# A hybrid block with a sparse mixture of experts: tokens sorted on the chip, and two of four tiles combined and gated between the last expert units

## The reference

```
v   = rmsnorm(h)
moe = for each token: the best of 4 groups of experts, in it the best 2 of 8 experts,
      expert(v) = (silu(v @ w_gate) * (v @ w_up)) @ w_down        # 1024 -> 256 -> 1024
      weighted by the group's probability and the two experts' weights
h   = h + moe
gate = sigmoid(rmsnorm(h) @ W_g + b_g)                            # W_g: 1024 x 1024
h   = h + gate * (p @ W_ple)                                      # p: 512 x 256
out = rmsnorm(h)
```

## Time and profile before

| | us |
|---|---|
| median of 3 runs | 517.59 (516.82 to 517.95) |
| the profiled execution's own time | 518.2 |
| its span | 516.5 |
| busy: TensorE / VectorE / ScalarE / GpSimd | 461.3 / 227.3 / 164.7 / 146.9 |
| DMA, mean over the span | 280 GB/s, 144.86 MB |

### The profile page before, as it was taken

How to read it: one execution, slowest core, us unless ns; L and a number is a source line. 1 busy time by engine, 2 the same in 40 slices (tenths; PEclk the granted TensorE clock), 3 DMA queues, 4 the chain that set the end, 5 groups by cost and what they waited for, 6 DMA issues and landing times. The chain is left out here.

```text
span 516.5 us, 9292 instructions
## 1 busy us (share of the span) xinstructions
PE 461.3 (89%) x3673; PEld 244.9 (47%) x3673; DVE 227.3 (44%) x685; ACT 164.7 (32%) x272; POOL 146.9 (28%) x133
## 2 busy tenths in 40 slices
PE   3799999999999999999999999879967668699993
PEld 3355555744844468655444454434423223344441
DVE  2899949999133358542222222213201000654525
ACT  5633576547342334011111111121200012113464
POOL 1069999615100001342322222102200000003250
PEclk9999999999999999999999999989978789799997
DMA  8784200399499967899999999999999999930022
GB/s 301 141 206 91 63 0 2 147 142 203 159 340 418 420 287 267 303 383 422 414 416 418 419 413 415 419 421 417 418 421 420 423 415 390 397 125 0 1 81 81
DMA packets 59636, 144.86 MB, mean 280 GB/s; under 512 B 27058, under 2 KB 36326, under 8 KB 47304
## 3 DMA queue, kind: packets, MB, share of 16 engines
q1 hardware_dynamic: 54504, 133.90, 70.4%
q0 software_dynamic: 4816, 10.32, 5.2%
q10 hardware_dynamic: 272, 0.04, 0.0%
HBM read 137.10 MB, written 13.15 MB: 291 GB/s over the span
## 5 line engine op out<-in xcount | busy, mean ns | idle before, releaser
L1759 PE MATMUL bank<-ring,moe 128*32 128x256 f32 (+2 forms) x1424 | 105.3, 427 | 16.4 <-DMA ring<-in_exp_w_up_dram 9.8
L1759 PEld LDWEIGHTS bank<-ring,moe 128*32 128x32 f32 (+1 forms) x1424 | 52.3, 119 | 58.1 <-issue 18.0
L965 DVE TENSOR_TENSOR vrow<-moe,bank 64x128 f32<-64x128 f32 x56 | 16.3, 291 | 140.9 <-ACT moe L872 140.1
L1674 POOL DMA_INDIRECT pairs_d<-moe,sidx_all x28 | 27.8, 993 | 148.9 <-ACT moe L601 91.5
L1759 PE MATMUL bank<-ut,big 128*128 128x512 f32 x128 | 57.7, 597 | 2.1 <-ACT ut L613 2.1
L1759 PE MATMUL bank<-ring,ut 128*128 128x512 f32 x128 | 57.6, 609 | 0.0
L872 ACT ACTIVATE moe<-bank 64x256 f32<-64x256 f32 x28 | 10.6, 377 | 144.4 <-PE bank L1759 144.4
L601 ACT ACTIVATE moe<-bank 128x512 f32<-128x512 f32 (+1 forms) x61 | 34.1, 581 | 60.2 <-PE bank L1759 47.4
L1759 PE MATMUL bank<-big,moe 128*32 128x256 f32 (+1 forms) x416 | 42.3, 454 | 7.2 <-DMA h<-in_exp_w_up_dram 3.4
L965 DVE TENSOR_TENSOR ring<-ring,bank 128x64 f32<-128x64 f32 (+1 forms) x142 | 39.3, 277 | 2.8
L1759 PEld LDWEIGHTS bank<-ring,ut 128*128 128x128 f32 x128 | 24.8, 197 | 30.2 <-issue 30.2
(11 more groups left out here) (224 smaller groups left out, 603.8 us busy)
## 6 DMA issues: line engine op xcount, KB each, us to landing
ring<-in_exp_w_gate_dram SPq DMA_DIRECT2D x21, 1024.0 KB, 21.4
ring<-in_exp_w_up_dram SPq DMA_DIRECT2D x18, 1024.0 KB, 23.3
ring<-in_exp_w_down_dram SPq DMA_DIRECT2D x15, 1024.0 KB, 23.7
big<-in_exp_w_down_dram SPq DMA_DIRECT2D x9, 1024.0 KB, 23.3
big<-in_exp_w_up_dram SPq DMA_DIRECT2D x6, 1024.0 KB, 18.4
big<-in_exp_w_gate_dram SPq DMA_DIRECT2D x5, 1024.0 KB, 17.3
h<-in_exp_w_up_dram SPq DMA_DIRECT2D x4, 1024.0 KB, 26.1
zbuf<-in_exp_w_gate_dram SPq DMA_DIRECT2D x3, 1024.0 KB, 19.4
```

Of the source, the lines that this page charges most:

```text
L965: return dve.tensor_tensor(o, a, b, op)
L1674: pool.indirect_dma_start(pairs, bass.IndirectOffsetOnAxis(ap=index, axis=0), at(moe, ALL, M_Y + k * 512, [[1, 512]]), None, bounds_check= ...
L1759: return pe.matmul(o, a, b, start=start, stop=stop, skip_group_check=loose)
```

## The change

- Tokens get a new order for the tail. A token that uses none of the eight experts of units 24 to 27 is put in front (`classes`, `positions` on VectorE and TensorE: a mask product, a running count over the tokens by matmul). Tiles 0 and 1 are then 256 tokens whose results are complete after unit 23.
- The positions are used by GpSimd: at unit 4 it scatters each token's two weights, its root and its number to its position in HBM (`posaux_d`), at unit 6 it reads them back; `inverted` (VectorE, unit 9) takes the token numbers as row indices `inv_i`.
- All rows of the tail go by these indices: p is gathered by GpSimd at unit 12, pairs and h by `fetch(t)` (two indirect DMAs), and the output tiles are scattered by GpSimd (`give`), the last in halves. SyncE does none of these any more. ScalarE issues the loads of the two vectors.
- `fetch(0)` and `fetch(1)` follow unit 23's scatter, after waiting for all scatters to land; VectorE sums tile 0 (`early_sum(0)`) after its step of unit 24, TensorE transposes it and does product 0 after the hidden transposes of unit 25, product 1 after unit 26's gate/up product. Tile 1 follows one unit later. Their gate rows, roots and sigmoids stand in the same places on VectorE and ScalarE.
- Scaling by the root is applied to the sum (`scaled_sum`, one operation more per half for tiles 0 and 1); for tiles 2 and 3 it is in `late_sum`, which also adds the placed rows, so `combined` and `spread` are left for two tiles. Units 24 and 25 are scattered as before; where two scatters of zeros filled the rows of units 26 and 27, four now fill those of units 24 to 27.
- The gate's weights are loaded inside the weight stream, ahead of pieces 82 and 86, into places 0 to 3 of the ring, which end their use as weight places at piece 60 and after. So do places 18, 20 and 21 (and 16 and 17 at piece 38, 19 at 76). From piece 77 on a piece follows the one that used its place at a distance of 11, later 10 (18 before).
- p x W_ple moves: `P_ROWS` from 19 to 15, `P_PROJ` to (17, 19, 21, 23).

```diff
@@ places, SyncE @@
+        KEPT = {10: 22, 11: 22, 16: 38, 17: 38, 0: 60, 1: 60, 2: 60, 3: 60, 18: 58, 20: 60, 19: 76, 21: 61}
-            kept = (SPOT[q] in (10, 11) and q >= NPIECE) or (SPOT[q] in (16, 17) and q >= 52)
-            if len(SPOT) < 3 * NE and not kept:
+            if len(SPOT) < 3 * NE and q < KEPT.get(SPOT[q], 3 * NE):
...
+        G_LOAD = (82, 86)
...
+                if p == G_LOAD[0]:
+                    sp.wait_ge(gu_ps, 23)
+                    sp.wait_ge(dn_ps, 22)
+                    load_gate(0, ld_wple)
+                if p == G_LOAD[1]:
+                    load_gate(1, ld_wple1)
...
@@ ScalarE @@
+                if e == 24:
+                    norm3(0)
+                if e == 25:
+                    norm3(1)
+                    for n in range(3):
+                        sigmoid(n)
+            sigmoid(3)
...
+            norm3(2)
+            norm4(0)
+            norm4(1)
+            norm3(NT - 1)
+            sigmoid(4)
+            sigmoid(5)
+            warm(2)
+            norm4(2)
             sigmoid(2 * NT - 2)
...
@@ VectorE @@
+            def classes():
+
+                own.do(dve.memset(at(rw, ALL, RW_E + NT, [[1, 1]]), 0.0))
+                seq(tt(qv("pb", te), qv("MS", te), at(bank[7], ALL, PS_LOW, [[0, NT], [1, NE]]), ALU.mult))
+                peak(at(rw, ALL, RW_E, one), qv("pb", te))
+                dve.tensor_scalar(at(rw, ALL, RW_E, one), at(rw, ALL, RW_E, one), 0.0, None, ALU.is_equal
+                                  ).then_inc(sort_sb, 1)
...
+            def pairs_added(t):
+
+                dve.wait_ge(ld_pairs[t], 32)
+                for n in range(2):
+                    pair_added(t, n, 0).then_inc(comb, 1)
+                    dve.wait_ge(comb, paired(t, n) + 1)
+                    pair_added(t, n, 1).then_inc(comb, 1)
...
             for e in range(NU):
                 step(e)
+                if e == 2:
+                    positions()
+                if e == 9:
+                    inverted()
+                if e == 24:
+                    early_sum(0)
+                if e == 25:
+                    turned_g_ple(0)
+                    root3(0)
+                    dve.wait_ge(ld_bias, BIAS_IN)
+                    gate(0)
+                    early_sum(1)
+                if e == 26:
+                    gate(1)
+                    turned_g_ple(1)
+                    root3(1)
+                    gate(2)
+                if e == 27:
+                    gate(3)
...
+            pairs_added(2)
+            pairs_added(3)
+            late_sum(2)
+            turned_g_ple(2)
+            root3(2)
+            late_sum(3)
+            root4(0)
+            root4(1)
+            root3(3)
+            gate(4)
+            turned_g_ple(3)
+            final(0)
+            gate(5)
+            final(1)
+            gate(6)
+            gated_sum(6)
+            root4(2)
+            final(2)
...
@@ GpSimd @@
+            def fetch(t, done):
+
+                home, off = pairs_at(t)
+                for o, rows in ((at(home, ALL, off, [[1, 2 * DM]]), pair_rows), (at(h, ALL, t * DM, [[1, DM]]), v_d)):
+                    pool.indirect_dma_start(o, None, rows, bass.IndirectOffsetOnAxis(ap=inv_i[:, t:t + 1], axis=0),
+                                            bounds_check=T - 1, oob_is_err=False).then_inc(done, 16)
...
+                if e == 23:
+                    for k in range(YBUF):
+                        pool.wait_ge(ys_stored[k], 16 * len(range(k, e + 1, YBUF)) + 16 * LOW // 2 * (k == 2))
+                    pool.wait_ge(pp_ps, 2 * NT)
+                    for t in range(EARLY):
+                        fetch(t, ld_pairs[t])
...
+            pool.wait_ge(gu_ps, 26)
+            pool.wait_ge(dn_ps, 26)
+            for t in range(EARLY, NT):
+                fetch(t, ld_pairs[t])
...
+            for n in range(2 * EARLY):
+                gated_sum(n)
+            for t in range(EARLY):
+                pool.wait_ge(fin_done, t + 1)
+                give(out_d, inv_i[:, t:t + 1], T - 1, t, 0, DM)
+            for n in range(2 * EARLY, 2 * NA):
+                gated_sum(n)
+            pool.wait_ge(fin_done, NA)
+            give(out_d, inv_i[:, NA - 1:NA], T - 1, NA - 1, 0, DM)
+            for n in range(2):
+                pool.wait_ge(fin_done, NT + n)
+                give(out_half, out_i[:, n:n + 1], 2 * T - 1, NA, n * 512, 512)
...
@@ TensorE @@
             for e in range(1, NU):
                 if e > 1:
                     h_step(e)
+                if e == 25:
+                    early_turned(0)
+                    pe.wait_ge(ld_wple, WPLE_IN)
+                    gate(0)
+                if e == 26:
+                    early_turned(1)
+                    gate(2)
...
                 if e + 1 < NU:
                     gu_step(e + 1)
+                if e == 1:
+                    positions()
...
+                if e == 25:
+                    pe.wait_ge(ld_wple1, WPLE1_IN)
+                    gate(1)
+                if e == 26:
+                    gate(3)
                 down_step(e)
...
-            for t in range(NT):
+            pe.wait_ge(gate_in, 2 * EARLY)
+            for t in range(EARLY, NT):
                 combined(t)
...
+            turned_h(2)
+            gate(4)
+            turned_h(3)
+            for n in range(5, 2 * NT):
+                gate(n)
```

426 lines of the change are left out of this document (244 added, 182 removed).

## The result

The changed kernel takes **520.4 us** (median; 519.67 to 520.88), the kernel before 517.4 on the same chip: a ratio of 1.0057, 95% interval 1.0039 to 1.0074. That is slower by 0.6%, where 512.1 us and faster was forecast, and outside the range of 504.5 to 518.5. The profiled execution's span is 518.9 us (before 516.5), its own time 520.6.

The account below looks back on a forecast made before the run. Last units DMA-bound, tail TensorE-bound; four products move into TensorE's idle time. Span 498.0 + 1.4 + 8.04 + 3.2 + 0.3 = 511.0 us against 516.5, so median 517.6 - 5.5 = 512.1 us; range 504.5 to 518.5.

Parts of the forecast that it names:

- GpSimd's order, delay of gate row 7: Tail: GpSimd's gated sums of tile 2 stand behind output tile 1's scatter, 29.7 against 28.35 us, so +1.4.
- 8.04 + 3.2 us: After the last product: 8.04 us to the span's end as before, plus 3.2 for storing the last rows by GpSimd scatters.
- a scatter that lands in 6.83 us: Before tile 0's fetch: GpSimd goes on 6.83 us after unit 23's scatter starts, as at unit 25, so at 395.3.
- The rates: Tile 0's fetch on the software queue: 0.13 MB/us for 4 KB rows of h, 0.17 for 8 KB rows of pairs.
- VectorE's order now decides: Ahead of product 4: VectorE's copy, gate row 3, eight additions and late sum set its start, at 469.7 us.
- The price of the scatters, +3.2: Output end: two GpSimd scatters, the second issued 0.6 us later than SyncE's, landing in 5.7 us instead of 3.1.
- The bound of +5 for the output: Upper bound on the added time of the last rows leaving by GpSimd scatters; bounds +1 and +5 us.
- The weights have slack: Weight stream, last units: last gate/up piece at about 441 us, against 444.
- Rival A: Tile 0's fetch is quick, landing at 403.4, all behind it 6.6 us earlier: median 505.5 us, chance 0.22.
- Rival C: Longer tail chain: VectorE's additions, GpSimd's gated sums and output scatters over the sum, about 515 to 518 us, chance 0.09.
- Rival B: Tile 0's fetch: software queue gets under its third; at 0.09 MB/us it lands at 417.1, median 519.2 us, chance 0.13.
- rival D: Weight stream starves with only ten pieces in reach, products end DMA-bound at the old pace: about 517 us, chance 0.04.

Follow-up runs that it names:

- the run with the sums reordered: Changed kernel with GpSimd's gated sums of tile 2 ahead of the scatter of output tile 1: 517.5 us (1.0005).
- the plain stores: Changed kernel with output tiles stored by plain SyncE DMAs instead of GpSimd's scatters: 515.2 us; also without GpSimd's waits for the scaled tiles: 512.6 us.

## Why the prediction was wrong, point by point

| step (us in the span) | forecast | measured |
|---|---|---|
| GpSimd goes on after unit 23's scatter | 395.3 | 397.39 |
| tile 0 landed | 410 | 412.67 |
| TensorE takes up unit 25's transposes | 414.7 | 417.15 |
| product 0 starts | 416.3 | 419.36 |
| product 0, its duration | 9.0 | 9.22 |
| product 2 | 440.0 | 442.98 |
| product 3 | 450.4 | 453.64 |
| down of unit 27 | 460.4 | 463.27 |
| product 4 | 469.7 | 474.53 |
| last product ends | 498.0 | 503.14 |
| GpSimd's order, delay of gate row 7 | +1.4 | +1.54 |
| from there to the end | 11.2 | 14.2 |
| span | 511.0 | 518.9 |

**What held.** VectorE blocks for tile 0, TensorE idles 14.2 us, from there it is the bound, no weight is waited for at units 26 and 27, the last four products run without a gap, and GpSimd's sums of tile 2 come 1.5 us late.

**What failed.** A gain of 5.5 us was forecast and the span grew by 2.4. The 7.9 us between them are three steps of the sum. The end was counted as 8.04 + 3.2 us, with GpSimd's closing drain at nothing; because of it the program ended 4.3 us after SyncE was through (3.0 us over the sum). The fetch was counted from a scatter that lands in 6.83 us; it took 8.34 (with the rest of the fetch, 3.0 us at product 0). And ahead of product 4 VectorE was taken for the path, where it was TensorE's own combination (1.9 us).

**The fetch, 3.0 us.** Two thirds arose before it began: unit 23's scatter started 0.6 us later, and from its start to the first fetch it was 8.34 us where the rows of unit 25's scatter gave 6.83. The fetch itself took 15.3 us from there, 14.7 forecast, and that it is so near is partly luck. The rates were put too low: with rows of 8 KB the queue had 55.9% in 403:405, 0.23 MB/us instead of 0.17. And without the bias load (the run with it later) it had 43.0 and 47.3% in the two windows from 405 to 409, 0.19 MB/us, with rows of mostly 4 KB, where the sum took 0.13 for these:

```profile
q0 software_dynamic: 78, 0.35, 43.0%
...
q0 software_dynamic: 79, 0.39, 47.3%
```

But the bias load of ScalarE, for which the sum had no term, took 25.9% there and left the software queue 34.7%, 0.14 MB/us. Two errors of opposite sign. (By the Trainium skill, DMA: Bandwidth & Descriptors, "Queues, rings and completion order", the engines take turns between queues; a third queue that lowers the shares of the others agrees with that. By the same page's "Anatomy of one DMA — SWDGE (gpsimd) path", 2.0 us + bytes/436 GB/s, which the prediction had weighed, one would estimate tile 0 at about 403; it came at 412.67.)

**The combination ahead of product 4, 1.9 us.** "VectorE's order now decides" was wrong by a little. The transposes of tile 2 stand on TensorE right behind the combination, which began 2.52 us after the down product of unit 27 and took 5.4 us (467.71 to 473.1) at a granted clock of 0.54 for the first 3.3 us; the sum had no term for it. VectorE's first half of the late sum was ready at about 472.5, some 0.6 us sooner. VectorE was late as well (its second group of four additions took 4.87 us beside GpSimd's gated sums, not 2.99 + 1.0): where the combination ran at full clock, in the run with the sums reordered, TensorE waited 0.59 us for it, and product 4 came 10.7 us behind the down product instead of 11.3 (forecast 9.3). So the clock is 0.5 of the 1.9 us, and VectorE's own lateness is the next bound under it.

**The end, 3.0 us.** The price of the scatters, +3.2, was nearly right in sum: from VectorE's last pair to the end the changed kernel takes 10.1 us and the plain stores 7.6, so 2.5. Its terms were not: the landing was put at 5.7 us from the issue, by a gather in the full stream, and took 2.7, while the last issue came 1.4 us later than SyncE's (2.8 against 1.4 us after VectorE's last pair began), not 0.6. What was missing is that GpSimd must still close its program behind its last wait. In the kernel before it did so from 500.7 on, and no row of the tail that was read showed it; the plain stores with and without GpSimd's waits differ by 2.7 us in the medians and 3.4 in the profiled ends. The bound of +5 for the output did not cover it (10.1 against 3.8 before is +6.2), and the prediction's range neither.

**"The weights have slack" was wrong**, though it didn't decide the sign. The last gate/up piece came at 444.5, where 441 was forecast, unit 26's at 424.3, and the gate's second half at 430. Rival A, worth 7 us and 0.22 of the chance, was built on it: "nothing else needs the engines' whole time". Fetched 14.1 us sooner the tile brought 1.6. With that, little stood behind the range below 510. Rival C, a longer tail, came in part. Rival B did not come: its mechanism was a software queue under its third, and the queue had more (34.7 to 55.9%); the rows were late mostly because the scatter ahead of them was.

**Shallow places (rival D)** did not starve the stream: the DMA share is 1.02 from 399 to 440, and 0.96 in 385:399.

**Clock and profile.** The forecast took 0.6 us between profile and median; it was 0.2. Product 0 was put at 9.0 us and took 9.22, but four profiles of nearly the same code have 7.87 to 8.85, so the agreement is partly luck. The 59.7 us of the earlier trace rows hold the transposes of three tiles, 3 x 8, not 8 x 8; that changes nothing in the sum.

## What to carry to other kernels

When work moves into a gap, the loads that it needs move too, and into a stream that is full: here 13.7 us of later weights, 11.2 us of sums and combination without cover and 7.7 us more at the end stood against 30.2 us of earlier products, and behind the wait that was costed stood another bound 1.4 to 2 us away. Two bounds that lie level show themselves only when both are removed. In this kernel the engine that was given the last output work also took its closing drain to the end of the program: leave GpSimd's last wait early, or count the drain; and put work that others wait for ahead of stores that nobody waits for.

## What the runs showed of the hardware that was not expected

- GpSimd's closing drain lasted 5.4 us with its last wait long past (7.0 in the plain stores without waits), 4.1 with a late wait and no transfer of its own, 5.6 in the changed kernel with plain stores, 7.1 and 7.9 with one and two scatters in flight (these two include the last issues). VectorE's lasted 1.45, SyncE's 7 ns. In these runs it starts only when the engine's waits are done, and the program doesn't end before it.
- Indirect fetches with rows of 8 KB had 56% of the DMA engines beside a full weight stream, with rows of mostly 4 KB 43 to 47%, where a scatter had 32%; a load of 0.5 MB on a third queue took 26%, and left the software queue 35%.
- After a scatter of a 128 x 512 tile in the full stream GpSimd waited 7.4 us more for the landing; at the end of the kernel, with nothing beside it, one of the same shape took 2.7 us from issue to landing (median of two).
- Four additions of 512 columns: 2.99 us on VectorE alone, 4.87 beside two operations of GpSimd.
- The first gate product behind 14 to 16 us of an idle TensorE took 7.87 to 9.22 us in five profiles with the same code ahead of it, 7.13 at full clock: a profile of one execution can differ by 1.4 us in this alone.
